# Modulation steps moved into the first dense product, and a quartered TensorE array for the RWKV pairs, in a hybrid RWKV-7 / mLSTM / PEER step

## The chip, the cores and the metric

The kernel runs on one core of a Trainium2 chip. The metric is the device time of one execution in microseconds (us), lower is better. The core has TensorE (PE, matrix products), VectorE (DVE), ScalarE (ACT), GpSimd (POOL) and SyncE (SP), which here only issues transfers. The engines run their own instruction streams in order and meet at semaphores.

## The reference

One layer of a decoder trunk on 288 tokens: 256 of a prompt and 8 sequences of 4 sample tokens. D is 2048. A conditioning vector c per sequence (9 in all) gives six modulation vectors for the layer and two for the end, each by a 2048 x 2048 matrix product.

```python
mod = silu(c) @ w_ada + b_ada          # six parts of 2048
sh_a, sc_a, g_a, sh_c, sc_c, g_c = split(mod, 6)
h = rmsnorm(x, g) * (1 + sc_a) + sh_a
z = h @ w_in                           # RWKV part, mLSTM q/k, mLSTM v/o/gates
y_a = rwkv7(z_a)                       # 16 heads of 64, delta rule, one step per token
y_b = mlstm(z_qk, z_rest)              # 4 heads, q/k 128 wide, v 256 wide
x += g_a * (concat(y_a, y_b) @ w_out)
h = rmsnorm(x, g2) * (1 + sc_c) + sh_c
x += g_c * peer(h)                     # 128 x 128 experts, top 16 in each of 8 heads
y = rmsnorm(x, g3) * (1 + sc_f) + sh_f # sh_f, sc_f from silu(c) @ w_ada_final
```

The RWKV step of a head is S = S diag(d) + (S (-kk)) (kk a)^T + v k^T, y = S r, with d the decay. Of the six modulation vectors only sh_a and sc_a are needed before the first product; g_a is needed after w_out, the others later still.

## The kernel before, in words

**Tiles and ring.** All weights come as tiles of 1 MB (128 partitions x 2048 words) through a ring of four slots. SyncE loads tile n when the semaphore `used` says that tile n - 4 has been used (`load`, `ada`). There are 32 modulation tiles at the front (parts SC_A and SH_A, 16 each), 50 tiles of w_in, 96 modulation tiles (G_A, SH_C, SC_C, G_C, SH_F, SC_F), 16 of w_out, 16 of w_q and 256 of the experts.

**A dense tile** (`dense`) multiplies a weight tile with 288 tokens in two halves of precision: ScalarE copies the tile to its high half (`hi`, two instructions), POOL subtracts that from the tile and gets the low half (`lo`, two instructions), and PE does 16 x 3 matmuls of 128 x 128 by 128 x 288 (high x high, high x low, low x high). In w_in the high halves have two buffers. ScalarE's queue has per tile: wait for the matmuls of tile j, `hi` of tile j + 2, then the copy of tile j out of its bank. For the first eight tiles (mLSTM q and k) the copy is followed by a wait for VectorE's convolution and a sigmoid. The loop over w_in has bodies of four tiles.

**A modulation step** (`ada_step`) takes one tile of 512 rows x 512 columns: 16 float32 matmuls with 32 columns of silu(c) as weights, in four column groups of the array. A float32 matmul stands in the trace as two records, so a step is 32 records. Four steps make a row of results that ScalarE copies out (`ada_take`); four such rows are folded to one part (`ada_turn`, 8 records) and stored (`ada_store`). The 96 deferred steps are put by hand, `ada_more(count)`, at places of the mLSTM and RWKV stages: 4 and 3 before the heads, 7 in each of four mLSTM heads, 11 until the RWKV pairs, 20 and 21 in the two pairs, 9 after them. PE's queue holds them in program order between the other matmuls.

**mLSTM heads.** For each head: products for the numerators (three banks), nine state updates (PE fills bank 4 or 5, VectorE takes it; update u waits for VectorE's update u - 2), the scores of the next head, and one sum of squares. The steps stood two after update 1, one after update 4, one after the scores, three after the sum.

**RWKV pairs.** The prompt has four chunks of 64 tokens, taken in two pairs: chunk j of a pair is on partitions 64j to 64j + 63, for all 16 heads. Grams and tokens come first; then the inverse of a triangular matrix per head by six levels of doubling:

```python
def times(bank, q, lhsT, rhs):        # heads 8q to 8q+7
    for h in range(8 * q, 8 * q + 8):
        for j in range(2):
            mm = matmul(ps[bank][PART[j], ...], lhsT[PART[j], h, :], rhs[PART[j], h, :])
```

A level is X = mask x Ti (`times` to banks 0 and 1), ScalarE's copies of X, then Ti += Tt X (banks 2 and 3) and Tt += X Tt (banks 0 and 1), added by VectorE in two halves of eight heads. Each `times` is 64 records for 16 heads. A head's matmul has its rows (its operands' partitions) and its columns (the partitions of its output) both in half j, so that two of the four quarters of the array are used, each pair of them writing the same bank. The products with AV (`akv`, `pu`) are placed alike. The products with PU (`mr`, state update, parts) take rows by chunk and columns by head. A step stood before and after the second half of every level.

POOL makes the mask of level i once level i - 2's X is done, and in the first pair three further products between them.

## Time and profile before

| | |
|---|---|
| median of 3 runs | 2926.09 us (2925.2 to 2926.27) |
| profiled execution | 2921.68 us, span 2919.9 us |
| PE busy | 2725.9 us of the span, 93% |
| POOL, VectorE, ScalarE busy | 1771.7, 1121.3, 951.9 us |
| read from and written to memory | 518.77 MB, 23.84 MB |
| granted PE clock, mean | 0.955 |

Stages, in us from the span's start: modulation parts 1 and 2 until 124; w_in 124 to 455; mLSTM until 618; preparation of the RWKV operands until 659; pairs 659 to 744 and 744 to 843; the sample tokens and the norm until 945; w_out and w_q until about 1175; the experts to the end. Granted clock 1.00 is 2.4 GHz and a mean between 0.5 and 1 mixes the two levels of 2.4 and 1.2 GHz.

How to read the rows below: a timeline row is start, duration, engine, line, instruction, out<-in with shapes, count, and in brackets the idle time before it with what ended it. PE rows carry `128*32` for the weights' shape; nearly all have line 701, the helper that issues a matmul. `kept` is the lower part of on-chip memory with the ring, `staged` the upper, `bank` a PSUM bank. "issue" means that the engine waited for nothing that the profile shows.

### The profile page before, as it was taken

How to read it: one execution, taken by the hardware profiler on the slowest of the kernel's cores; microseconds unless marked ns; L12 is line 12 of the kernel's file. 1: busy time of each engine (PE TensorE's matmuls, PEld its weight loads, DVE VectorE, ACT ScalarE, POOL GpSimd, SP SyncE). 2: the span in 40 equal slices, each digit the busy share in tenths (PEclk: the TensorE clock that was granted, in tenths of full speed). 3: DMA queues.
4: the chain of work that ended last, by engine and by line, in shares of the span. 5: the costliest groups of instructions: out<-in, count | busy, mean ns of one | idle time of the engine just before them, and what ended most of it. 6: DMA issues, size and time to landing. Idle time of an engine off the chain costs nothing.

```text
span 2919.9 us, 62759 instructions
## 1 busy us (share of the span) xinstructions
PE 2725.9 (93%) x25899; PEld 2620.6 (90%) x25899; DVE 1121.3 (38%) x2241; ACT 951.9 (33%) x1353; POOL 1771.7 (61%) x745
## 2 busy tenths in 40 slices
PE   5789999979875989999999999999999999999997
PEld 3689997768763979899999999999999999999997
DVE  0450664464237120896477313200131101455134
ACT  1343432131112333444333333333333333332333
POOL 0267771003211677688655577777777777888775
PEclk9899997679986999999999999999999999999999
DMA  9744445888664434344455444555544555554442
GB/s 374 263 142 165 165 160 212 290 294 285 233 208 162 159 126 162 130 158 158 174 182 181 164 171 159 179 185 187 177 159 172 184 182 189 185 183 174 169 163 104
DMA packets 150467, 544.94 MB, mean 187 GB/s; under 512 B 8984, under 2 KB 18856, under 8 KB 121512
## 3 DMA queue, kind: packets, MB, share of 16 engines
q1 hardware_dynamic: 136672, 505.18, 49.0%
q10 hardware_dynamic: 11480, 20.44, 1.9%
q0 software_dynamic: 2160, 17.03, 1.5%
q8 instruction: 125, 2.05, 0.3%
q14 instruction: 30, 0.25, 0.0%
HBM read 518.77 MB, written 23.84 MB: 186 GB/s over the span
## 4 chain that ended last, share of the span: by engine, by line
issue 39%; POOL 35%; PE 21%; DVE 3%; ACT 1%; POOLq 1%; DMA 0%; DVEq 0%; ACTq 0%
POOL ring_lo L605 34%; PE bank L701 21%; PE bank L704 0%; DVE staged L2106 0%; DVE y_lo L1758 0%; DMA kept<-in_w_ada 0%; POOLq L604 0%; DVE staged L2059 0%; ACT hi_peer L1337 0%; POOLq L609 0%; DVE staged L2093 0%; POOL h_lo L675 0%; POOL staged L694 0%; DVE staged L2095 0%; POOL staged L683 0%
## 5 line engine op out<-in xcount | busy, mean ns | idle before, releaser
L605 POOL TENSOR_TENSOR ring_lo<-kept,hi_peer 128x1024 fp32r<-128x1024 f32 x576 | 1441.6, 2526 | 496.9 <-ACT hi_peer L1337 496.9
L1337 ACT ACTIVATE hi_peer<-kept 128x1024 fp32r<-128x1024 f32 x576 | 578.1, 1051 | 1134.0 <-PE bank L701 1133.9
L701 PE MATMUL bank<-h_hi,ring_lo 128*128 128x288 f32 x3104 | 914.0, 294 | 0.0
L701 PE MATMUL bank<-h_hi,hi_peer 128*128 128x288 f32 x2304 | 686.1, 298 | 18.1 <-DVE h_lo L2152 10.3
L701 PE MATMUL bank<-h_lo,hi_peer 128*128 128x288 f32 x2304 | 680.7, 295 | 0.0
L701 PE MATMUL bank<-act_hi,hi_peer 128*128 128x288 f32 x2048 | 604.8, 295 | 6.7 <-POOL ring_lo L605 3.6
L701 PE MATMUL bank<-act_hi,ring_lo 128*128 128x288 f32 x2048 | 604.5, 295 | 0.0
L701 PE MATMUL bank<-act_lo,hi_peer 128*128 128x288 f32 x2048 | 604.2, 295 | 0.0
L701 PEld LDWEIGHTS bank<-h_hi,ring_lo 128*128 128x128 f32 x3104 | 585.8, 189 | 0.0
L701 PEld LDWEIGHTS bank<-h_hi,hi_peer 128*128 128x128 f32 x2304 | 432.4, 188 | 21.4 <-issue 16.2
L701 PEld LDWEIGHTS bank<-h_lo,hi_peer 128*128 128x128 f32 x2304 | 433.3, 188 | 0.0
L701 PEld LDWEIGHTS bank<-act_hi,hi_peer 128*128 128x128 f32 x2048 | 384.8, 188 | 8.4 <-POOL ring_lo L605 8.4
L701 PE MATMUL bank<-staged 64*64 64x64 f32 (+10 forms) x5264 | 339.9, 267 | 52.6 <-issue 18.3
L701 PEld LDWEIGHTS bank<-act_hi,ring_lo 128*128 128x128 f32 x2048 | 385.1, 188 | 0.0
L701 PEld LDWEIGHTS bank<-act_lo,hi_peer 128*128 128x128 f32 x2048 | 384.9, 188 | 0.0
L701 PEld LDWEIGHTS bank<-staged 64*64 64x64 f32 (+5 forms) x5264 | 283.3, 153 | 102.4 <-issue 51.8
L605 POOL TENSOR_TENSOR ring_lo<-kept,hi_front 128x1024 fp32r<-128x1024 f32 x100 | 243.3, 2453 | 205.1 <-ACT hi_front L1337 205.1
L2273 DVE CAST act_hi<-staged 128x576 fp32r<-128x576 f32 (+1 forms) x128 | 84.9, 663 | 578.1 <-PE bank L701 578.1
L701 PE MATMUL bank<-h_hi,hi_front 128*128 128x288 f32 x800 | 236.4, 296 | 11.4 <-POOL ring_lo L605 11.4
L701 PE MATMUL bank<-h_lo,hi_front 128*128 128x288 f32 x800 | 236.7, 296 | 0.0
L701 PE MATMUL bank<-kept,staged 128*32 128x128 f32 x4144 | 176.9, 328 | 64.0 <-DMA kept<-in_w_ada 36.9
L701 PEld LDWEIGHTS bank<-kept,staged 128*32 128x32 f32 x4144 | 137.9, 132 | 98.4 <-DMA kept<-in_w_ada 44.5
(219 smaller groups left out, 2371.0 us busy)
## 6 DMA issues: line engine op xcount, KB each, us to landing
kept<-in_peer_u SPq DMA_DIRECT2D x128, 1024.0 KB, 4.7
kept<-in_peer_v SPq DMA_DIRECT2D x128, 1024.0 KB, 5.5
kept<-in_w_ada SPq DMA_DIRECT2D x96, 1024.0 KB, 8.6
kept<-in_w_in SPq DMA_DIRECT2D x50, 1024.0 KB, 4.7
kept<-in_w_adaf SPq DMA_DIRECT2D x32, 1024.0 KB, 5.6
kept<-in_w_out SPq DMA_DIRECT2D x16, 1024.0 KB, 4.8
kept<-in_w_q SPq DMA_DIRECT2D x16, 1024.0 KB, 4.7
gates_spill<-staged ACTq DMA_DIRECT2D x24, 576.0 KB, 3.0
```

What stands on the lines that cost most here:

```text
L605: pool.tensor_tensor(ring_lo[:, n % RING_SLOTS, cols], ring[n % RING_SLOTS][:, cols], hi_slot(n)[:, cols].bitcast(F32), ALU.subtract).then ...
L701: return pe.matmul(out, lhsT, rhs, start=start, stop=stop)
L1337: return act.activation(out, in_, ACT.Copy)
L2273: dve.tensor_copy(act_hi[:, n % 2], a).then_inc(S("acts_hi"), 1)
```

## The change

First edit. Parts G_A and SH_C (32 tiles) leave the ring's later order and get two buffers of their own, `early`. Eight bodies of the w_in loop (now a loop of eight and one of four, where there were two of six) each take four steps: in the middle of tile 0, after tile 0, after tile 1, in the middle of tile 2; after tile 3 one fold of the row (`early_turn`). ScalarE takes the row before it waits for tile 3 (`early_take`). SyncE's queue interleaves the loads. 64 steps stay deferred: 2 in each head (5 fewer), 14 and 15 in the pairs (one per level, before the second half), the others as they were.

Second edit. In the pairs, heads are split into even and odd in place of lower and upper eight. For odd heads Ti, X-to-Tt products, AV and Tt have their chunks on the other half of the partitions (`side`), so that a product's output of an odd head lies in the other half from its operands, in a bank of its own. For this level 0 gets 16 matmuls with the unit matrix that bring the odd heads' mask over (into bank 3), and the last token turn becomes 12 matmuls where there were 4 transposes. X goes to banks 4 and 5. Both halves' waits are joined: a level's first product waits for both additions to Ti, the second for both copies of X. The products with PU go through their four combinations of chunk and head in the order `TILES`.

```diff
-        wg_hi, wg_lo = parts("wg_hi", za, KT, 36), parts("wg_lo", za + KT * 36, KT, 36)
+        early = [words(q5 + D + KT * N + b * D, D) for b in range(2)]
+        TILES = ((0, 0), (1, 1), (0, 1), (1, 0))
+        def side(h, j):
+            return PART[j ^ h % 2]
...
+            def load_early(q, body, i=0):
+                if q >= 2 or body or not isinstance(i, int):
+                    sp.wait_ge(S("early_used"), i * 4 + (4 * body + q - 1))
+                sp.dma_start(early[q % 2].rearrange("p (k c) -> p k c", k=4),
+                             T["w_ada"][q * 512:(q + 1) * 512, cols].rearrange("(k p) c -> p k c", p=P)
+                             ).then_inc(S(f"early{q % 2}_landed"), 16)
+            def load_body(z_j, z_at, body, last=False, i=0):
+                load_early(2, body, i)
+                load_z(z_j, z_at, i)
+                load_early(3, body, i)
+                load_z(z_j + 1, z_at + 1, i)
+                if not last:
+                    load_early(0, body + 1, i)
+                    load_early(1, body + 1, i)
+                load_z(z_j + 2, z_at + 2, i)
+                load_z(z_j + 3, z_at + 3, i)
...
+            def early_step(i, q):
+                pe.wait_ge(S(f"early{q % 2}_landed"), i * 32 + 16 * (q // 2 + 1))
+                if q == 0:
+                    pe.wait_ge(S("ada_copied"), i + 8)
+                for k_ in range(4):
+                    for g in range(4):
+                        mm = matmul(ps[6][32 * g:32 * g + 32, 0:P], silc[:, 4 * q + k_, :],
+                                    early[q % 2][:, k_ * 512 + g * P:k_ * 512 + (g + 1) * P],
+                                    q == k_ == 0, q == k_ == 3)
+                mm.then_inc(S("early_used"), 1)
+            def early_turn(i):
+                pe.wait_ge(S("ada_copied"), i + 9)
+                matmul(ps[7][:, bass.ds(i * (4 * NS), 4 * NS)], early_row, cst1("fold")).then_inc(S("ada_turned"), 1)
...
-            with pe.Fori(0, 6) as i:
+            with pe.Fori(0, EARLY_BODIES) as i:
                 for j in range(4):
                     pe.wait_ge(S("z_free"), i * 4 + (j + 1))
-                    dense(n_z + j, h_hi, h_lo, i, j % 2, "h")
+                    dense(n_z + j, h_hi, h_lo, i, j % 2, "h", {0: 0, 2: 3}.get(j))
+                    if j < 2:
+                        early_step(i, j + 1)
+                early_turn(i)
...
-                    if u in (1, 4):
-                        ada_more(2 if u == 1 else 1)
...
-                ada_more(3)
+                ada_more(1)
...
+                def times(bank, lhsT, rhs, rows, out, count):
+                    for h in range(AH):
+                        for j in range(2):
+                            mm = matmul(ps[bank + h % 2][out(h, j), (h // 2) * L:(h // 2 + 1) * L], lhsT[rows(h, j), h, :],
+                                        rhs[rows(h, j), h, :])
+                            if h >= AH - 2 and j == 1:
+                                mm.then_inc(S(count), 1)
...
+                    times(4, mk[i % 2], Ti, here, side, "x_sum")
+                    ada_more(1)
+                    pe.wait_ge(S("x_copied"), x_copies(p, i, 1))
+                    pe.wait_ge(S("t_added"), T_ADDS * p + 4 * i)
+                    if i < LEVELS - 1:
+                        times(2, Tt, X, side, here, "t_sum")
+                    times(0, X, Tt, side, side, "t_sum")
...
+            def early_take(i, first):
+                act.wait_ge(S("early_used"), i * 4 + 4 * (first + 1))
+                act.wait_ge(S("ada_turned"), i + (first + 5))
+                copy(early_row, ps[6][:, 0:P]).then_inc(S("ada_copied"), 1)
...
                 for j in range(4):
+                    if j == 3:
+                        early_take(i, 0)
                     act.wait_ge(used, i * 4 + (n_z + j + 1))
```

## Rows read from the trace of the kernel before

**Rows 1.** The page: busy tenths of PE and its granted clock, 40 slices of 73 us.
```profile
PE   5789999979875989999999999999999999999997
PEclk9899997679986999999999999999999999999999
```

**Rows 2.** Stretches: window, PE, PEld, DVE, ACT, POOL busy, PE clock, DMA share, GB/s.
```profile
199.00:455.20 256.20, 252.76 (x1921) 252.37 (x1921) 102.94 (x113) 100.04 (x177) 194.20 (x80) 1.00 0.46 164
522.40:555.00 32.60, 32.17 (x319) 24.51 (x315) 17.29 (x41) 5.01 (x9) 1.61 (x3) 0.69 0.89 322
659.00:744.00 85.00, 76.14 (x2214) 69.19 (x2216) 32.68 (x44) 14.87 (x29) 26.46 (x11) 0.94 0.78 264
700.00:721.00 21.00, 21.00 (x681) 19.41 (x678) 8.28 (x11) 4.14 (x8) 13.94 (x5) 1.00 0.77 258
744.00:843.00 99.00, 87.60 (x2410) 77.68 (x2406) 27.72 (x44) 18.93 (x39) 18.76 (x10) 0.95 0.69 227
868.00:880.00 12.00, 8.07 (x426) 6.83 (x416) 2.58 (x2) 1.27 (x5) 0.00 (x0) 0.80 0.06 18
1440.00:1480.00 40.00, 40.00 (x318) 40.00 (x317) 29.67 (x83) 14.04 (x24) 21.13 (x9) 1.00 0.50 183
```

**Rows 3.** Waits of PE, 124 to 205 us: total us, times, longest.
```profile
PE bank L701 <- POOL ring_lo L605: 9.3, 7, 2.7
```

**Rows 4.** Timeline of ScalarE in the convolution tiles.
```profile
156.24 1.99 ACT L1337 ACTIVATE hi_front<-kept 128x1024 fp32r<-128x1024 f32 x2
...
163.69 0.46 ACT L1334 ACTIVATE staged<-staged 128x312 f32<-128x312 f32 x1 [4.99 <-DVE staged L1807]
...
165.47 1.06 ACT L1337 ACTIVATE hi_front<-kept 128x1024 fp32r<-128x1024 f32 x1
```

**Rows 5.** Timeline of the second mLSTM head: modulation steps, an update by VectorE, a fold.
```profile
533.36 3.64 PE L701 MATMUL bank<-kept,staged 128*32 128x128 f32 x64
...
536.09 0.48 DVE L1936 SCALAR_TENSOR_TENSOR staged<-staged,bank 128x256 f32<-128x256 f32 x1
...
540.00 1.94 PE L701 MATMUL bank<-kept,staged 128*32 128x128 f32 x32
...
550.54 1.95 PE L701 MATMUL bank<-kept,staged 128*32 128x128 f32 x64
...
552.43 1.08 PE L701 MATMUL bank<-staged 128*128 128x36 f32 x8
```

**Rows 6.** Waits of PE, 455 to 945 us: total us, times, longest.
```profile
PE bank L701 <- issue: 27.8, 19, 4.7
...
PE bank L701 <- DMA kept<-in_w_ada: 5.8, 2, 5.2
```

**Rows 7.** Timeline of PE after the pairs.
```profile
871.22 1.92 PE L701 MATMUL bank<-staged 64*32 64x64 f32 x128 [0.37 <-issue]
874.70 1.84 PE L701 MATMUL bank<-staged 64*32 64x64 f32 x128 [1.56 <-issue]
```

**Rows 8.** PE's instruction queue, 659 to 744 and 1400 to 1600 us: packets, MB, share.
```profile
q8 instruction: 17, 0.28, 1.3%
...
q8 instruction: 4, 0.07, 0.1%
```

**Rows 9.** Timeline of PE in the first pair: step, products by times, state update.
```profile
693.12 1.08 PE L701 MATMUL bank<-kept,staged 128*32 128x128 f32 x32
694.13 2.08 PE L701 MATMUL bank<-staged 64*64 64x64 f32 x64
...
697.16 3.95 PE L701 MATMUL bank<-staged 64*64 64x64 f32 x128
...
702.05 2.08 PE L701 MATMUL bank<-staged 64*64 64x64 f32 x64
...
735.13 2.02 PE L701 MATMUL bank<-staged 64*64 64x64 f32 x117 [1.29 <-issue]
```

**Rows 10.** The page's transfers of w_ada: count, KB each, us to landing.
```profile
kept<-in_w_ada SPq DMA_DIRECT2D x96, 1024.0 KB, 8.6
```

More of the change, by code:

```diff
@@ L503, in parts_turned, with parts_stored @@
         def parts_turned(j):
-            return j + 4 if j else 1
+            return j + 10 if j else 1
+        def parts_stored(j):
+            return j + 3 if j else 1
+        EARLY_BODIES = 8
         ada_places = []
@@ L738, in ada_step @@
                 mm.then_inc(used, 1)
-                if quarter == 0 and j > 0 and j != 2 and q == 3:
+                if quarter == 0 and (j == 1 or j > 4) and q == 3:
                     ada_turn(j - 1)
@@ L752, in ada_more, with dense @@
                     ada_step(*pending.pop(0))
-            def dense(n, hi, lo, i, bank, split=None):
+            def dense(n, hi, lo, i, bank, split=None, middle=None):
                 w_hi, w_lo = hi_slot(n), ring_lo[:, n % RING_SLOTS]
                 for kt in range(KT):
+                    if kt == 8 and middle is not None:
+                        early_step(i, middle)
                     if kt % 8 == 0:
@@ L1047, in _ @@
+                    for j, hp in TILES:
+                        h = 2 * f + hp
+                        out = ps[2 + j][PART[hp], f * AHD:(f + 1) * AHD]
+                        mm = matmul(out, ktok2[PART[j], h, :], vtok2[PART[j], h, :], False, p == j == 0 and f == MT - 1)
                 if p == 0:
                     mm.then_inc(S("step_ready"), 1)
-                else:
-                    pe.wait_ge(S("rk_taken"), MT)
                 ada_more(1)
@@ L1355, in ada_store @@
                      turn_bank(j)[:, 0:KT * NS]).then_inc(S("mods_raw"), 1)
-            pending = [(j, q) for j in range(2, 8) for q in range(4)]
+            pending = [(j, q) for j in range(4, 8) for q in range(4)]
             ada_steps = [0]
@@ L1474, in take_z @@
                 copy(zxs[:, j % 2, :, 0], src).then_inc(S("zx_full"), 1)
-            with act.Fori(0, 6) as i:
+            with act.Fori(0, 2) as i:
+                for j in range(4):
+                    if j == 3:
+                        early_take(i, 6)
+                    take_z(i, j, j)
+            act.wait_ge(S("ada_turned"), 13)
+            copy(mods[:, G_A:G_A + 2].rearrange("p m k s -> p (m k s)"), ps[7][:, 0:2 * KT * NS]).then_inc(S("mods_raw"), 1)
+            with act.Fori(2, 6) as i:
                 for j in range(4):
@@ L1561, in _ @@
                         act.wait_ge(S("x_sum"), x_sums(p, i, q))
[L1562 removed]
+                        copy(X[:, q::2], ps[4 + q][:, :].rearrange("p (h t) -> p h t", h=8)).then_inc(S("x_copied"), 1)
                     if p == 1 and i >= 2:
```

229 lines of the change are left out of this document (124 added, 105 removed).

## The prediction

> **What bounds the kernel now.** The page comes first: TensorE (PE) is busy nearly throughout, with a dip between 455 and 945 us (slices 7 to 13 of 40, 73 us each), where the granted clock also falls [rows 1]. The table of stretches then splits the front half [rows 2]. The sum is made against the profiled execution, 2921.68 us (span 2919.9); the median of the runs, 2926.09 us, stands 4.4 us above it, and I add that back at the end.
>
> In the first dense product (124 to 455.2 us, 50 tiles) PE is the bound except in its first 75 us: from 199 to 455.2 it is idle 3.4 of 256.2 us, at full clock, with the DMA engines 46% busy [rows 2]. In the first 75 us, the eight convolution tiles, PE waits seven times for the low halves of the weights, 9.3 us in all [rows 3]. What is late there is ScalarE: it can take the next tile's high half only after the previous tile's sigmoid, which waits 5.0 us for VectorE. Its loop takes 7.9 us per tile (it starts a high half at 156.24 and ends the sigmoid of that turn at 164.16) [rows 4], against 6.3 us of matmuls (later in the stage 1921 records fill 252.8 us, 0.132 each, 48 to a tile [rows 2]).
>
> In the mLSTM heads (488 to 618 us, some 32.5 us each) PE is busy but mostly at half clock (0.69 in the second head) [rows 2]. The row of one head shows what a modulation step costs: two in a row 3.64 us at half clock, one alone 1.94, two at full clock 1.95 [rows 5].
>
> In the two RWKV pairs (659 to 843 us) PE is nearly saturated, with gaps that the view calls issue: 27.8 us of them in 455 to 945, 19 times, the largest cause in this stretch; the transfers of w_ada cost PE only 5.8 us [rows 6]. I read the issue gaps as instruction fetch, and two rows show its floor: two runs of exactly 128 matmul records start 3.48 us apart, though each ran only 1.92 and 1.84 us, with a gap of 1.56 between, in a stretch where the DMA engines are 6% busy [rows 2, 7]. The first pair issues 2214 matmul records while PE's instruction queue brings 17 packets, 130 records to a packet [rows 2, 8]. I call 128 records a page (256 instructions, with their weight loads): fetch supplies a page in no less than about 3.45 us.
>
> **The first edit: 32 of the 96 steps move.** Each dense body of four tiles gets four steps and one small fold; eight bodies.
> Price of a step: one at full clock between other work starts 1.01 us before what follows it (693.12 to 694.13) [rows 9].
> - Bodies 2 to 7 lie where PE never waits. 24 x 1.01 = 24.2 us, all on the path. The fold is two records; eight of them take 1.08 us [rows 5], so 6 x 0.27 = 1.6.
> - Bodies 0 and 1 lie where PE has 9.3 us of waits. Eight steps (8.1) fit, but the fold waits for ScalarE's copy of the finished row, which stands behind the third tile's sigmoid in ScalarE's queue. ScalarE starts its turn for the fourth tile at 156.24; PE's fourth tile should be through at about 149.5 (its high half starts two turns earlier, near 140.5, and POOL's two subtractions and the second half of the matmuls end some 9 us after that). So PE stands there about 7 us, with the fifth tile behind it, and then finds both halves of that tile ready. It catches up before ScalarE needs it: tile 4 ends near 164.2 and ScalarE turns to it at 165.47. Going through both bodies like this, tile 10 ends about 5.2 us later than now, four of which are body 2's own steps. I charge 1.2 us.
> - Transfers: SyncE's queue gets four more loads of 1 MB per body, interleaved with the weights. A body then moves 8.39 MB in 4 x 6.3 + 4.3 = 29.5 us, 284 GB/s; the table shows 322 GB/s in the second head [rows 2]. A weight tile has two tiles of time (12.6 us) between its load and ScalarE's first read of it; even the w_ada loads of now land in a median of 8.6 us [rows 10]. The tightest early tile is asked for at the middle of tile 0 and used after tile 1, some 10.5 us later. I take nothing, and keep the shortfall as a rival. POOL's queue is not touched; ScalarE gets eight copies of 0.28 us, hidden where it is not the bound.
> Sum for the dense stage: +27 us. Bounds: 22 (7 of the 9.3 us hide, steps at the 0.94 us that they take in a row) and 34 (each step 0.2 us dearer, for emptying the array at both changes of shape, and no cover).
>
> The Trainium skill, TensorEngine Tiling (Array Packing), section Tiling Modes, says that changing the tiling mode drains TensorE. No row prices a drain inside a dense tile; the difference between 1.01 and 0.94 us is what this trace shows of it, and by the page's rule the sum would lie nearer the 34.
>
> **What leaves the heads** (5 of 7 steps in each of four). The two steps after the first two updates cover a wait that stays: the third update needs VectorE's first, which it starts only at 536.09 and which needs a second small instruction behind its 0.48 us, while PE would be free at 533.36 [rows 5]. Worth nothing. The step after the fifth update (1.94 us) has no wait behind it, and two of the three at the tail (0.98 each, full clock) have none either, since the next head's scores are ready before. 4 x (1.94 + 1.95) = 15.6, I take 16. Below, 12: the lighter load keeps the clock low. Above, 22: the shorter tail carries the high clock further into the next head.
> With 20 tiles fewer asked for, the ring is full at the end of the heads: the 5.8 us of waits for w_ada go, and with them the cold steps behind the 5.22 us one (1.94 us at half clock against 1.08). -8 (5 to 11).
>
> **The pairs.** Three things change. One of two steps per level goes (6 per pair, 192 records each pair). The products by `times`, `akv` and `pu` use four quarters of the array instead of two. Level 0 gets 32 records by the unit matrix, the last token turns 16 more records per half.
> What four quarters give: two-quarter products take 3.95 us per 128 records, 30.9 ns each; the state update, whose order already visits all four, takes 2.02 us for 117, 17.3 ns [rows 9]. If nothing else bound, a full level would go from 7.92 us (694.13 to 702.05 [rows 9]) to 1.1 + 1.0 + 2.2 plus two waits that one step no longer hides, about 0.5 each, for ScalarE's two copies and VectorE's two additions: 5.3 us.
> But a level still has 64 + 32 + 128 = 224 records, 1.75 pages, and fetch gives a page in 3.45 us at best, so 6.0 us. The first pair now takes 85 us for 2214 records, 17.3 pages: 4.9 us per page; the second 99 for 2410, 18.8 pages: 5.3 [rows 2]. After: 192 - 32 - 32 = 128 records fewer in each, exactly one page. From 700 to 721 a page took 3.95 us without a gap under 77% DMA [rows 2]. I take 3.95 for the first pair (16.3 x 3.95 = 64, and 6 for waits on VectorE: 70, -15) and 4.3 for the second (17.8 x 4.3 + 6 = 82.5, -16). Together -31. Bounds: -10 if pages keep today's pace (one page each), -40 if the dependence alone decides.
>
> **Sum.** +27 - 16 - 8 - 31 = -28. Profiled 2921.7 - 28 = 2894; as a median 2926.1 - 28 = **2898 us**. What follows 843 us is unchanged. The likeliest case's own range is 2872 to 2914.
>
> **Rivals.** Less than about 0.2% (6 us) can't be told from no change here.
> 1. Fetch eats the second edit: pages keep 4.9 and 5.3 us, the pairs give 10 only, net -7: 2919 us. For it: 19 gaps of some 1.5 us stand in the middle stages [rows 6], under 69% DMA in the second pair. Against: 3.95 us held for 21 us, and halving the steps eases the DMA engines. A part of this is that the quarters don't run side by side (the change doesn't do what it says); the update's 17.3 ns speaks against that. Chance 0.18.
> 2. The dense loop no longer fits PE's instruction store. Its body grows from 384 to 640 matmul and weight-load instructions, two and a half pages. If each of seven returns to the loop's head waits for a page, 7 x 3.5 to 5.3 us, up to 37: net -4 to +9, about 2929. Against: the loop with the gates (4 x (96 + 48) = 576 instructions, 2.25 pages) runs from 1400 to 1600 us with four instruction packets in the whole 200 us [rows 8], and PE is busy in 40 of the 40 us of one pass [rows 2]. Chance 0.07.
> 3. The other side: the early tiles come too late. The dense stage is fed at 164 GB/s now. If the mixture with w_ada reached only the 227 GB/s of the second pair, a body would take 37 us, not 29.5: 6 x 7.8 = 47 on top, net +19, 2945 us. It decides from the point where six bodies lose 28 us, 34.2 us a body or 245 GB/s. Against: 322 GB/s with the same tiles in a later stretch. Chance 0.07.
> 4. More than forecast: pairs -40, heads -22 with full clock, dense +24: below 2872. Chance 0.05.
> That leaves 0.63 for the forecast.
>
> The Trainium skill, Runtime: NRT & Kernel Launch, section Instruction fetch mechanics, says that a taken branch whose target lies outside a window of two pages forces a fetch; by that rule rival 2 would be the outcome. The same section gives PE an instruction memory of 2048 instructions, by which it would not. The four packets of the gates' loop side with the second.
>
> **Chances and range.** Faster by over 0.2%: the forecast, rival 4 and a good half of rival 1, 0.78. Within 0.2%: the rest of rival 1 and part of 2, 0.09. Slower: most of 2 and rival 3, 0.13. The range of 8 in 10 runs from 2868 to rival 1 with 2 us to spare, 2921.
>
> **What would show it.** Right: the dense stage ends about 27 us later, with no DMA waits in it and 32 groups of 32 records among the dense ones; the second head shorter by 4 us with a new wait of some 3.5 us for VectorE before the third update; no wait for w_ada near 614; `times` at 16 to 20 ns a record with issue gaps that fill part of what that saves; the pairs near 70 and 83 us. Wrong: instruction packets in the dense stage, waits for the early tiles, pairs above 80 and 94 us, or a half clock in the dense bodies.

## The result and the profile after

The changed kernel takes 2941.08 us (median of 13 runs, 2929.75 to 2944.91), the kernel before 2924.11 us beside it: a ratio of 1.0057, 95% interval 1.0047 to 1.0067. It is slower by 17 us where I had forecast 28 us less. Of all the executions in this document one, of experiment 1, ran in a slow state (3071.55 us, against 2921.57 to 2925.73 for its eleven others), and its ratio leaves that one out. The profiled execution has a span of 2938.9 us, 19.0 more than before, and the stages below split those 19.0 us.

The page of the changed kernel, busy tenths of PE and its clock, in 40 slices of 73.5 us, answers to [rows 1]; PE is less busy in the slice where the first pair begins (the tenth, 7 tenths for 9), and the clock is lower in slices 9 to 11 (6, 8 and 8 tenths for 7, 9 and 9).

```profile
PE   4799999887875989999999999999999999999997
...
PEclk9899998668886999999999999999999999999999
```

Four rows of the changed kernel answer to [rows 2]: the stretch of the dense product, most of the one between it and the pairs, and each pair from its first gram to its last product (window, busy us and instructions of PE, PEld, DVE, ACT, POOL, PE clock, DMA share, GB/s).

```profile
200.00:492.00 292.00, 292.00 (x2774) 283.35 (x2774) 100.40 (x118) 104.15 (x188) 195.20 (x80) 1.00 0.66 227
492.00:660.00 168.00, 144.76 (x1070) 106.98 (x1070) 84.17 (x181) 31.82 (x60) 8.80 (x16) 0.64 0.48 174
681.27:768.39 87.12, 71.44 (x2129) 62.65 (x2129) 30.76 (x42) 14.26 (x28) 26.43 (x11) 0.86 0.57 186
768.39:859.02 90.63, 76.08 (x2277) 65.52 (x2273) 27.75 (x43) 17.71 (x37) 19.95 (x10) 0.92 0.56 177
```

The kernel before, cut at the same places of its pairs:

```profile
660.29:745.22 84.93, 77.36 (x2249) 70.11 (x2249) 31.47 (x42) 15.46 (x30) 26.46 (x11) 0.94 0.78 265
745.22:844.05 98.83, 87.43 (x2404) 77.54 (x2401) 28.69 (x43) 18.93 (x39) 19.81 (x10) 0.95 0.68 226
```

PE's busy time in the pairs falls from 164.8 to 147.5 us, but its idle time rises from 19.0 to 30.2 us, and the first pair runs at a clock of 0.86 instead of 0.94. By stage, after less before:

| stage | before | after | difference | forecast |
|---|---|---|---|---|
| end of the dense product | 455.2 | 491.9 | +36.7 | +27 |
| from there to the first gram of the pairs | 205.1 | 189.4 | -15.7 | -24 |
| both pairs | 183.8 | 177.8 | -6.0 | -31 |
| from there to w_out's first matmul (944.58, 962.48) | 100.5 | 103.5 | +2.9 | 0 |
| rest | | | +1.1 | 0 |

The waits of PE from 120 to 500 us, changed kernel (total us, times, longest), answer to [rows 3]: ScalarE has taken POOL's place.

```profile
PE bank L747 <- ACT staged L1421: 8.3, 3, 3.0
```

Its timeline there: the wait of the first fold, in ScalarE's queue behind a sigmoid that waits for VectorE. ScalarE's copy of the fold row is the one at 157.40.

```profile
157.81 0.41 PE L747 MATMUL bank<-staged 128*128 128x36 f32 x2 [2.98 <-ACT staged L1421]
```
```profile
157.03 0.46 ACT L1418 ACTIVATE staged<-staged 128x312 f32<-128x312 f32 x1 [5.02 <-DVE staged L1907]
157.40 0.26 ACT L1421 ACTIVATE staged<-bank 128x128 f32<-128x128 f32 x1
```

A step inside a dense tile, changed kernel. Dense records follow one another 0.13 us apart; here the second record after the step starts 1.48 us after the last one before it, so the step costs 1.48 - 2 x 0.13 = 1.22 us. That is 1.01 us for the step itself (211.82 to 212.83) and 0.10 and 0.11 at its two ends, where the starts lie 0.23 and 0.24 us apart.

```profile
211.46 0.29 PE L747 MATMUL bank<-h_lo,hi_front 128*128 128x288 f32 x1
211.59 0.29 PE L747 MATMUL bank<-h_hi,ring_lo 128*128 128x288 f32 x1
211.82 1.08 PE L747 MATMUL bank<-staged 128*32 128x128 f32 x32
212.83 0.40 PE L747 MATMUL bank<-h_hi,hi_front 128*128 128x288 f32 x1
213.07 0.29 PE L747 MATMUL bank<-h_lo,hi_front 128*128 128x288 f32 x1
```

The waits of PE from 500 to 680 us: VectorE before each head's third update, as forecast, and w_ada, which was forecast to go.

```profile
PE bank L747 <- DVE staged L2037: 12.3, 4, 3.3
PE bank L747 <- DMA kept<-in_w_ada: 4.7, 1, 4.7
```

And the timeline of PE in the pairs of the changed kernel: the last token turn (with two steps in its group), the gaps, and what runs behind one.

```profile
692.37 6.99 PE L747 MATMUL bank<-kept,staged 128*128 128x64 f32 x112 [0.20 <-ACT staged L1421]
...
719.20 3.02 PE L747 MATMUL bank<-staged 64*64 64x64 f32 x128 [0.57 <-issue]
724.85 1.08 PE L747 MATMUL bank<-staged 64*64 64x64 f32 x45 [2.62 <-issue]
725.86 1.93 PE L747 MATMUL bank<-kept,staged 128*32 128x128 f32 x32
...
818.68 1.16 PE L747 MATMUL bank<-staged 64*64 64x64 f32 x64 [0.59 <-ACT staged L1421]
```

The quarters are faster, but not in every product: 64 records in 1.16 us are 18 ns each, and the two products behind them 3.02 us for 128, 23.6 ns, against 30.9 [rows 9]. These two are unlike, and the code says why:

```python
                    if i < LEVELS - 1:
                        times(2, Tt, X, side, here, "t_sum")
                    times(0, X, Tt, side, side, "t_sum")
```

The last two places before the name of the semaphore are the partitions of the operands and of the output. In `X Tt` an odd head's output lies in the same half as its operands, like an even head's. So this product still uses two quarters (as does the first product of level 0, by `here` for both), and the text on the second edit, which has a product's output of an odd head in the other half, does not hold for it. The trace shows it. The stretch of experiment 5 that has no gap splits into 0.98 us for the 64 records of `Tt X` and 1.84 us for those of `X Tt`, by the starts 15.3 and 28.8 ns a record. In experiment 8, with two quarters everywhere, the same two take 29.9 and 28.8. (Records that run over a cut are counted on both sides of it.)

```profile
711.76:712.74 0.98, 0.98 (x65) 0.98 (x66) 0.00 (x0) 0.00 (x0) 0.98 (x2) 1.00 1.04 408
712.74:714.58 1.84, 1.84 (x77) 1.84 (x68) 1.28 (x2) 0.00 (x0) 1.44 (x1) 1.00 0.33 124
```

And a page of 128 records that ran 3.02 us is followed by a gap of 2.62 us and then by a step at half clock (1.93 us, against 1.08 elsewhere).

### The profile page after: what moved, and what is told of

The parts are those of the page before. It is cut to its first block, busy times and chain, and to the rows that moved or that the text cites. A ratio compares the mean times of both kernels' runs of the same rounds, so it can differ in the third digit from the quotient of the medians.

```text
span 2938.9 us, 63158 instructions
## 1 busy us (share of the span) xinstructions
PE 2726.2 (93%) x26043; PEld 2613.6 (89%) x26043; DVE 1117.7 (38%) x2241; ACT 950.1 (32%) x1352; POOL 1772.5 (60%) x745
## 4 chain that ended last, share of the span: by engine, by line
issue 32%; POOL 31%; PE 26%; DVE 5%; DMA 3%; ACT 1%; POOLq 1%; SPq 0%; ACTq 0%; DVEq 0%
POOL ring_lo L651 31%; PE bank L747 26%; DMA kept<-in_w_ada 3%; DVE staged L1907 1%; ACT staged L1421 0%; DVE staged L2209 0%; PE bank L750 0%; ACT hi_front L1421 0%; DVE y_lo L1858 0%; DVE staged L1844 0%; POOLq L650 0%; DMA kept<-in_w_in 0%; DVE staged L2022 0%; DVE staged L2162 0%; ACT hi_peer L1421 0%
## 5 line engine op out<-in xcount | busy, mean ns | idle before, releaser
L747 PE MATMUL bank<-staged 64*64 64x64 f32 (+11 forms) x6352 | 361.1, 275 | 82.4 <-issue 29.7
L747 PEld LDWEIGHTS bank<-staged 64*64 64x64 f32 (+6 forms) x6352 | 296.6, 152 | 141.2 <-issue 75.0
L747 PE MATMUL bank<-kept,staged 128*32 128x128 f32 (+2 forms) x3216 | 150.5, 335 | 64.7 <-DMA kept<-in_w_ada 39.1
L1421 ACT ACTIVATE staged<-bank 128x384 f32<-128x384 f32 (+7 forms) x281 | 105.8, 417 | 288.1 <-PE bank L747 269.4
```

What stands on the lines that cost most here:

```text
L747: return pe.matmul(out, lhsT, rhs, start=start, stop=stop)
L1421: return act.activation(out, in_, ACT.Copy)
```

## The experiments

All ratios are to the kernel before, run beside on the same chip; the chips and the runs beside differ from experiment to experiment, so a difference of two medians can be off by some 3 us from that of the ratios. "Pairs" are the two spans from the profile of each, that is from one execution, cut as in the tables above.

**1 and 2. One edit at a time.** The first edit alone keeps the pairs of before, with one step per level (64 steps are left to place); the second alone keeps all 96 steps.

```diff
@@ first edit alone, against the changed kernel
-                    times(4, mk[i % 2], Ti, here, side, "x_sum")
+                        times(q, q, mk[i % 2], Ti).then_inc(S("x_sum"), 1)
...
@@ second edit alone, against the changed kernel
-            with pe.Fori(0, EARLY_BODIES) as i:
+            with pe.Fori(0, 6) as i:
                 for j in range(4):
-                    dense(n_z + j, h_hi, h_lo, i, j % 2, "h", {0: 0, 2: 3}.get(j))
+                    dense(n_z + j, h_hi, h_lo, i, j % 2, "h")
...
-                        ada_more(1)
+                        ada_more(2)
```

> The change with its second edit undone: steps beside the dense tiles, one step per level in the pairs, products on two quarters as before. The profile after has the dense stage 36.7 us longer and the stretch from its end to the first gram 15.7 us shorter. Theory F (fetch takes the second edit's gain): the pairs lose only the 12 steps, about three pages of instructions of 4.9 to 5.3 us, so 182.5 us go to about 170, and the total is the before plus 36.7 - 15.7 - 12 + 1 = +10 us. So the second edit by itself would cost some 6 us. Rival Q (the quarters do save what the matmul rate says, some 25 us, and something of the first edit costs it back): the pairs stay near 182 - 12 + 25 = 195 us and the total is +35 us.

Measured: 2923.61 against 2922.85 us, 1.0005 (0.9997 to 1.0014). Pairs 75.7 and 84.0 us.

> The kernel before with the second edit alone: all 96 deferred steps where they were, 7 in a head and two per level, products on four quarters. The dense stage and the heads should be as before to 1 us. Theory F: pages of instructions keep their pace, the pairs have 64 records each more than before (half a page) and the dearer token turn (2.4 us a pair in the profile after), so the pairs go from 182.5 to 183 to 190 us, total +1 to +8. Rival Q: 25 us saved, total -20 us.

Measured: 2940.53 us, 1.0057 (1.0043 to 1.0070). Pairs 96.5 and 105.9 us, in the slowest of its six executions (2946.41). The waits of PE, 655 to 870 us: the kernel before, the first edit alone, the second alone.

```profile
PE bank L701 <- issue: 23.6, 14, 4.7
```
```profile
PE bank L746 <- issue: 18.7, 13, 4.7
```
```profile
PE bank L702 <- issue: 33.2, 18, 3.3
```

So the second edit makes the whole loss, 18 us in the pairs, and it does so with the first edit (159.8 to 177.8) as without it (183.8 to 202.4; by the medians 17.5 and 17.7 us). The first edit is neutral: the 12 steps that leave the pairs give back 24 us there, two each, and not one. Both expectations for the second edit missed: one had it near nothing, the other at a gain.

**3. The fold row is taken early.** ScalarE copies the finished row right after it has handed the third tile to VectorE, before it waits for VectorE.

```diff
                 for j in range(4):
-                    if j == 3:
-                        early_take(i, 0)
...
                          conv0[:, bass.ds(i * 4 + j, 1)].rearrange("p o b t -> p (o b) t")).then_inc(S("zq_full"), 1)
+                    if j == 2:
+                        early_take(i, 0)
                     act.wait_ge(S("conv_ready"), i * 4 + (j + 1))
```

> The change with one thing moved: in the convolution tiles ScalarE copies the finished row in its turn for tile 2, ahead of the wait for VectorE's convolution, not at the head of its turn for tile 3. If the two waits of 3.0 us before the fold, and the half clock behind them (tile 8 took 3.1 us too long), cost what they look like, the dense stage ends 4 to 8 us earlier than in the change (its end at 491.9 us goes to 484 to 488) and the total is 4 to 8 us lower. Rival: ScalarE's loop is the bound there anyway, the time shows again as a wait for low halves, and only the cold 3 us come back, or nothing.

Measured: 2927.33 us, 1.0016 (1.0007 to 1.0025), 13.8 us less than the changed kernel by the medians and 12 us by the ratios (1.0057); the dense product ends at 481.2 instead of 491.9 and the first gram starts at 669.88 instead of 681.27. More than expected. The waits of PE, 120 to 500 us, now read:

```profile
PE bank L747 <- ACT staged L1421: 2.3, 1, 2.3
```

The two fold waits are gone, 6.0 us; the rest is what they did to the clock. In the changed kernel the first half of the tile behind each takes 4.8 and 5.8 us, with the row taken early 3.25 and 3.3, and the window up to 200 us has a clock of 0.91; with the row taken early it is 0.97:

```profile
120.00:200.00 80.00, 78.06 (x809) 73.43 (x810) 46.30 (x65) 32.06 (x58) 44.39 (x19) 0.97 0.77 269
```

**4. A quarter of the deferred loads.** Three of four loads of the 64 deferred tiles are left out; each step reads the quarter's one tile, so the modulations made from these tiles are not the reference's. Instructions on PE are the same.

```diff
-                    for q in range(4):
+                    for q in range(4 if j < 2 else 1):
...
-                n = ada_tile(j, quarter) + q
+                n = ada_tile(j, quarter) + (q if j < 2 else 0)
```

> The change, but of every four tiles of the 64 deferred modulation steps only one is loaded and used four times (three quarters of the rows of these weights are left out of the modulation vectors). PE issues the same instructions; the transfers of the middle stages fall from 67 to 17 MB. Theory L (instruction pages are late because they stand behind weight transfers): gaps called issue in the pairs shrink from some 30 us to below 12, a page comes in 3.5 us, and the pairs go from 177.7 to 155 to 162 us. Rival G (a page has a fixed latency of its own, or something else spaces it): the gaps stay, the pairs stay within 5 us. Either way the 4.7 us wait for w_ada at 640 goes.

Measured: 2909.11 us, 0.9961 (0.9948 to 0.9975). The wait for w_ada is gone and the first gram comes 5.5 us earlier (675.79); the pairs take 71.2 and 83.9 us with the DMA engines 16% and 20% busy. Theory L had the pairs right and the gaps wrong: the gaps called issue in 655 to 870 us add up to 19.7 us instead of 27.9, not to less than 12. Of the 22.7 us that the pairs lose, 12.2 are idle time of PE and 10.4 busy time, at a clock of 0.98 and 0.96 instead of 0.86 and 0.92. Two timelines show the same two products, 128 records in 3.02 us, and the start of what follows: with full loads (719.20 above) 5.65 us later, and here 4.00.

```profile
708.19 3.02 PE L747 MATMUL bank<-staged 64*64 64x64 f32 x128 [0.58 <-issue]
712.19 0.92 PE L747 MATMUL bank<-staged 64*64 64x64 f32 x45 [0.98 <-issue]
```

The same place in the second pair gives 5.91 us (795.61 to 801.52) and 3.72 (772.96 to 776.68).

The trace also has the time of every packet of PE's instruction queue, and these times tie the gaps to it. In the pairs of the changed kernel 17 gaps are called issue, and each of them ends 1.2 to 1.5 us after such a packet has landed; of this experiment's 17 in the pairs each ends 1.2 to 1.6 us after one. For the gap that ends at 724.85 the packet ran from 722.53 to 723.48, for the one at 712.19 from 709.81 to 710.69. The packet itself takes about 1.0 us in both kernels. What differs is when it starts: 3.3 and 3.6 us after the 128 records have begun (719.20, 795.61) under full loads, 1.6 and 1.1 us after (708.19, 772.96) under a quarter of them. So the gaps are instruction supply, and the transfers of w_ada slow it; at these places they delay the start of a packet, not its transfer.

**5 and 6. Four levels of the first pair, unrolled and in a loop.** In both, levels 1 to 4 go without their step (the four steps stand together behind them) and get four short matmuls that carry the waits; in one the four levels are written out, in the other they are two passes of a loop over two levels.

```diff
+                    pe.wait_ge(S("t_added"), it * 8 + (4 * (i - 1) + 3))
+                    carrier(4)
+                    times(4, mk[i % 2], Ti, here, side, "x_sum")
...
+                    with pe.Fori(0, 2) as it:
+                        for i in (1, 2):
+                            level(i, it)
+                    ada_more(4)
```

> The change, with the four steps of levels 1 to 4 of the first pair put behind level 4, and four small extra matmuls per level that carry the waits: the control for the next kernel, all instructions of the four levels written out. If fetch bounds them, the four levels (832 records, 6.5 pages with the extra ones) take 4.3 to 4.9 us a page, 28 to 32 us, with gaps called issue of 1 to 3 us each one or two pages. If the dependence through ScalarE and VectorE bounds them, they take about 4 x 5.5 = 22 us with waits on ScalarE and VectorE in place of the gaps.

> As the control, but levels 1 and 2 of the first pair are the body of a hardware loop that runs twice, so that the second pass (levels 3 and 4) needs no instructions from memory. Matmuls, waits, banks and transfers are the same. Theory F: the second pass has no issue gaps and takes about 2 x 5.5 = 11 us, against 14 to 16 in the control; the kernel is 3 to 6 us faster than the control. Rival D (dependence, not fetch): both passes take what they take in the control. Rival B: the return to the loop's head costs a gap of its own of 2 to 4 us.

Measured: unrolled 2939.54 us, 1.0065 (1.0039 to 1.0091); looped 2937.08, 1.0055 (1.0039 to 1.0072). The 2.5 us between them lie inside the intervals. The timelines say why there is nothing to gain: already unrolled, a level without a step has no issue gap, and yet the next one starts 6.92 us later, with waits for ScalarE (the copies of X) and VectorE (the additions).

```profile
711.20 0.62 PE L747 MATMUL bank<-kept,staged 128*32 128x128 f32 x4 [1.17 <-ACT staged L1447]
711.76 3.02 PE L747 MATMUL bank<-staged 64*64 64x64 f32 x128
714.70 0.41 PE L747 MATMUL bank<-kept,staged 128*32 128x128 f32 x2
715.45 0.41 PE L747 MATMUL bank<-kept,staged 128*32 128x128 f32 x2 [0.34 <-DVE staged L2143]
...
718.12 0.62 PE L747 MATMUL bank<-kept,staged 128*32 128x128 f32 x4 [1.17 <-ACT staged L1447]
```

These 6.9 us hold 0.9 us that the carriers put on the path: two of the four stand there for 0.56 us before the products (711.20 to 711.76) and the last for 0.33 us before the next level's first product (715.45 to 715.78). Without them a level is some 6.0 us, by my estimate: 1.2 for the first product, 1.2 until ScalarE's copies are done, 2.9 for the other two products, 0.75 until VectorE's additions are done. That, and not the 5.3 us of the prediction, is what the dependence of a level costs here. The loop could not show what supply costs, because its control had no gap left in these levels.

**7. The first edit alone with the fold row taken early.** Edit 3 on the kernel of experiment 1.

> The first edit alone (the pairs as before the change, but one step per level), with ScalarE's copy of the finished fold row moved ahead of its wait for VectorE in the two convolution bodies. The first edit alone came out at 1.0005 of the kernel before, and the move took 13.5 us off the changed kernel. If the two effects are independent, this one is 12 us faster than the kernel before (ratio 0.996), with pairs of about 76 and 84 us. Rival: the 13.5 us came partly from how the second edit's pairs met the transfers; then the move gives 4 to 8 us here and the ratio is 0.998.

Measured: 2911.4 us, 0.9966 (0.9953 to 0.9979), pairs 75.1 and 82.4 us. It is the fastest of all that compute the reference, 11.5 us under the kernel before, as the sum of the two effects said.

**8. Two quarters, same instructions.** On the kernel of experiment 3, the odd heads' products return to the partitions of the even ones (the products by the unit matrix in level 0 in the same way, not shown); number, order, waits and banks stay.

```diff
         def side(h, j):
-            return PART[j ^ h % 2]
+            return PART[j]
...
-    matmul(ps[4 + half][PART[1 - j], at + L:at + P], src[:, f, ct[j]], ident[:, L:P])
+    matmul(ps[4 + half][PART[j], at + L:at + P], src[:, f, ct[j]], ident[:, L:P])
```

> The changed kernel with the fold row taken early (2927 us, 1.0016), but every product of the odd heads is written on the same partitions as in the kernel before: number, order, waits and banks of all instructions stay those of the second edit, only the two products of a head with different result quarters become two with the same two quarters for all heads. Theory A (page supply sets the pace, the four quarters save nothing net): within 4 us of 2927, products by times at 31 ns a record instead of 18, issue gaps in 655 to 870 us down from 31 us to about 20, pairs of 84 to 89 us still. Rival B (the four quarters themselves lose the time, through the gaps and the half clock behind them): 8 us or more faster. Rival C (the four quarters do pay, the other parts of the second edit cost 30 us): 10 to 20 us slower.

Measured: 2928.57 us, 1.0020 (1.0007 to 1.0033), 1.2 us more than with four quarters, well inside the intervals. The gaps called issue in 655 to 870 us are 15.4 us instead of 31.2, fewer than the 20 expected. The pairs of the two, four quarters first:

```profile
669.88:754.90 85.02, 70.05 (x2129) 61.60 (x2129) 30.68 (x42) 14.26 (x28) 26.47 (x11) 0.88 0.59 190
754.90:843.48 88.58, 72.94 (x2277) 62.35 (x2273) 27.75 (x43) 17.71 (x37) 19.80 (x10) 0.98 0.58 181
```
```profile
670.20:758.11 87.91, 76.99 (x2128) 68.93 (x2128) 30.67 (x42) 14.26 (x28) 26.43 (x11) 0.94 0.57 186
758.11:849.99 91.88, 82.97 (x2276) 73.73 (x2272) 27.74 (x43) 17.71 (x37) 19.75 (x10) 0.96 0.55 173
```

The quarters take 17.0 us of busy time out of the pairs and put 10.8 us of idle time in; 6 us are left in these two profiles, 1 in the medians. Theory A.

**9. Two quarters, plain turns.** As 8, and the last token turn goes back to transposes (48 records become 8, not the 16 that I had counted: a transpose is one record here).

```diff
-                            if u < 3:
+                            if u <= 3:
                                 mm = turn(ps[4 + half][:, at:at + P], src[:, f, pt])
```

> As the one above, and the last token turn goes back to 16 matmul records by transposes (the 48 records of three matmuls per column block are gone). The turn's group took 6.99 us for 112 records, 64 of them two steps of 1.96 us, so 5.0 us against 2.5 us for the transposes: 5 us faster than the one above for two pairs if only its own records count (theory A), up to 10 us if it runs at half clock as in the second edit alone (9.39 us for the group) and its page no longer has to be fetched. If nothing (within 2 us), the turn was hidden by the supply of pages.

Measured: 2918.45 us, 0.9993 (0.9977 to 1.0009): 10 us less than experiment 8, pairs 82.1 and 89.8 us. The turn that moves the odd heads to their own partitions costs ten microseconds for two pairs, and its own records account for them. From the start of the turn to the end of the two steps behind it 8.58 and 6.92 us pass in experiment 8, and 2.96 us twice in experiment 9, 9.6 us less. Experiment 8, then the turn and the steps of the first pair in experiment 9:

```profile
679.75 8.65 PE L747 MATMUL bank<-kept,staged 128*128 128x64 f32 x112 [0.20 <-ACT staged L1421]
...
767.66 6.99 PE L747 MATMUL bank<-kept,staged 128*128 128x64 f32 x112 [0.20 <-ACT staged L1421]
```
```profile
679.58 1.15 PE L750 MATMUL bank<-kept,staged 128*128 128x128 f32 x8 [0.20 <-ACT staged L1421]
680.65 1.95 PE L747 MATMUL bank<-kept,staged 128*32 128x128 f32 x64
```

The expectation had set 5.0 us for the turn against 2.5 for the transposes. The transposes take 1.07 us (679.58 to 680.65), and the turn's group is 1.7 us longer where the clock falls in it (0.80 in the first pair, 1.00 in the second).

What is left of the second edit here (the other order of waits and of products, the other banks, 32 records of the unit matrix per pair) is 7 us against experiment 7 by the medians. The profiles say 14 us in the pairs, but the profiled execution here is the slowest of its twelve (2923.99). In the second pair the steps follow one another about 9.1 us apart instead of 8.0, and a wait for ScalarE stands in each level that shares its banks with the rk sums:

```profile
788.97 2.28 PE L747 MATMUL bank<-staged 64*64 64x64 f32 x64 [0.59 <-ACT staged L1421]
791.18 1.08 PE L747 MATMUL bank<-kept,staged 128*32 128x128 f32 x32
...
798.02 1.15 PE L747 MATMUL bank<-staged 64*64 64x64 f32 x32 [0.59 <-ACT staged L1421]
```

**10 and 11. The same pairs under a quarter of the loads.** The cut of experiment 4 on the first edit alone, and on the changed kernel with two quarters (outputs as there).

> The first edit alone, with three of four loads of the 64 deferred tiles left out (each step reads the quarter's one tile, so the output is not the reference's). To be held against the same cut in the changed kernel, 2909.1 us, pairs of 71.2 and 83.9 us. Theory A (pages come slower when the DMA engines are loaded, 5 us against 3.5 to 4.0 at 18% share, and the second edit costs its own extra records and colder turns whatever the load): pairs of 66 to 72 and 74 to 80 us, 2900 us or less. Rival (with cheap pages the four quarters pay): pairs longer than those of the changed kernel, 2915 us or more.

> The changed kernel with three of four loads of the 64 deferred tiles left out (2909.1 us, pairs of 71.2 and 83.9 us; output not the reference's), and the odd heads' products on the same partitions as the even ones', as in the run with two quarters and the same instructions. Theory A (the quarters pay only where pages come fast; under full load they gave nothing, 2928.6 against 2927.3): 5 to 12 us slower, pairs of 75 to 80 and 86 to 90 us. Rival N (the quarters pay nothing even then, waits between the engines eat them): within 3 us of 2909.

Measured: the first edit alone 2907.13 us, 0.9945 (0.9928 to 0.9962), pairs 72.3 and 81.9; the changed kernel with two quarters 2920.89 us, 0.9994 (0.9985 to 1.0003), pairs 80.5 and 88.6, against 2909.11 with four. Experiment 10 fell between its two expectations: with light loads the second edit costs 2 us by the medians and 4.7 by the ratios, where with full loads it costs 16 to 18. Experiment 11 says which part of it depends on the loads: four quarters (in all products but `X Tt`) are worth 11.8 us by the medians and 9.6 by the ratios when pages come fast, and 1.2 us, which can't be told from nothing, when they don't. Their pairs, four quarters first:

```profile
675.79:746.98 71.19, 63.79 (x2128) 55.95 (x2128) 30.58 (x42) 14.26 (x28) 26.50 (x11) 0.98 0.16 49
746.98:830.88 83.90, 73.29 (x2277) 63.02 (x2273) 27.73 (x43) 17.71 (x37) 19.80 (x10) 0.96 0.20 62
```
```profile
674.89:755.41 80.52, 76.14 (x2128) 68.87 (x2128) 30.64 (x42) 14.26 (x28) 26.45 (x11) 0.94 0.14 43
755.41:844.04 88.63, 81.62 (x2276) 72.43 (x2272) 27.74 (x43) 17.72 (x37) 19.77 (x10) 0.98 0.20 59
```

Busy time falls by 20.7 us and idle time rises by 6.6: the pairs keep 14.1 of it.

**12. The turn on quarters.** On experiment 3, the turn's matmuls use only the 64 partitions on which the head lies.

```diff
-    matmul(ps[4 + half][:, at:at + L], src[:, f, pt], ident[:, 0:L])
+    matmul(ps[4 + half][:, at:at + L], src[PART[0], f, pt], ident[PART[0], 0:L])
-    mm = matmul(ps[4 + half][PART[1 - j], at + L:at + P], src[:, f, ct[j]], ident[:, L:P])
+    mm = matmul(ps[4 + half][PART[1 - j], at + L:at + P], src[PART[1], f, ct[j]], ident[PART[1], L:P])
```

> The changed kernel with the fold row taken early (2927 us), four quarters kept, and the 48 records of the last token turn written as products that use only the 64 partitions on which a head lies: 16 on half of the array's rows and 32 on a quarter. Same number of records and instructions. In the two-quarter version the way back to 16 transposes gave 10 us. Theory T (the turn is dear because its matmuls run on whole columns, some 0.1 to 0.2 us each, and chill the clock): the group of 112 records falls from about 7 to 9 us to 4 us, and the kernel by 6 to 10 us, to 2917 to 2921 us; it stays above the 2911 us of the first edit with the early row, since the four quarters save nothing there. Rival S (what the way back to transposes gave was the 32 records fewer, a quarter of a page): group shorter, but the pairs within 2 us of 85.0 and 88.6 us.

Measured: 2930.1 us, 1.0025 (1.0013 to 1.0038), 2.8 us more than experiment 3, not 6 to 10 less. Both theories missed: the group of 112 records still takes 8.56 and 9.86 us, and the pairs 91.1 and 92.6 us, in an execution at the slow end of its eight (2934.59).

```profile
679.64 8.56 PE L747 MATMUL bank<-kept,staged 64*128 64x64 f32 x112 [0.20 <-ACT staged L1421]
```

In the changed kernel the 48 records of a turn take 5.0 us at full clock, 105 ns each. The six of a block start 0.16, 0.21, 0.01, 0.10, 0.01 and 0.15 us apart, and here, on 64 partitions, just the same to 0.01 us. The 0.21 stands behind the product with 128 columns and the 0.15 ahead of the next one, the others have 64; no run took these changes away, so why the turn is dear stays open. Its share of the array is not the reason.

## Why the prediction was wrong

**Dense stage, bodies 2 to 7: mechanism right, size off.** The term was 24 x 1.01 + 1.6 = 25.8 us. The folds of the changed kernel stand 30.24 us apart, and four tiles of before take 192 x 0.1316 = 25.27 [rows 2], so a body gained 4.97 us and six of them 29.8. The price of a step there is 1.22 us, not 1.01: some 0.1 us at each change between whole and narrow columns. It lies inside the bound of 34. The Trainium skill, TensorEngine Tiling (Array Packing), section Tiling Modes, has it that a change of tiling mode drains TensorE; I had kept it for the upper bound only, and the trace agrees that the change costs something, 0.21 us a step.

**Bodies 0 and 1: the step that failed first.** I wrote that PE stands some 7 us at the fold, finds both halves of the next tile ready and catches up, and charged 1.2 us. Measured: 36.7 - 29.8 = 6.9 us at the end of the dense product. With the row taken early (experiment 3) it ends 10.7 us sooner, 25.9 us after that of the kernel before, so that the two bodies then give back 3.9 us. The waits were shorter than I thought, 2.98 us twice, 6.0 of the 10.7. What I left out is the clock: the work with which PE was to catch up ran partly at half speed behind each wait, 4.0 us in the two half tiles.

**The loops.** Rival 2 did not come: between 124 and 492 us PE's instruction queue brings 5 packets, though the dense body is more than 640 instructions long. The page of the Trainium skill that I weighed, Runtime: NRT & Kernel Launch, section Instruction fetch mechanics, fits this stage with its 2048 instructions and not with its window of two pages. Rival 3 did not come either: no wait for a transfer in the stage, at 227 GB/s with every tile in time.

**Heads: right.** The third updates stand 28.4, 28.5 and 27.6 us apart (541.91, 570.30, 598.80, 626.43) instead of some 32.5, so four heads give the 16 forecast or a little more, with the new wait for VectorE before the third update (3.31 us in three heads, 2.39 in the last).

**The w_ada wait: wrong.** I let 8 us go because the ring would be full, and even its rows give only 5.8 + 0.9 = 6.7. The wait of 4.74 us stays (645.15), at the fifth step of a row of five that takes 11 us, while the ring has four slots and a load lands in 8.8 us. That fewer tiles had been asked for before did not help; the wait was gone only with three of four deferred loads left out (experiment 4).

**Pairs: the step that decided.** -31 was forecast, -6 came, and of the two parts of the forecast one was too small and the other had the wrong sign. The 12 steps that leave give 24 us (experiment 1). I read this as 1 us of work and a quarter of a page to fetch for each, but their transfers leave with them, and no run separates the three. The second edit costs 18 us. Its failing step is "I take 3.95 for the first pair and 4.3 for the second": I took pages at 3.95 us without a gap [rows 2] as a proof that supply can do that, while they only show that work as long as that hides it. With work of 3.0 us a page, the next page came after 5.65 and 5.91 us. So the faster products turned into gaps (10.8 of 17.0 us, experiment 8). That gaps also cost clock shows in single rows (the 1.93 us step) and in the first pair, 0.88 with four quarters against 0.94 with two, but not in the second, 0.98 against 0.96. The second failing step is the level that would take 5.3 us if nothing else bound it: it takes some 6.0 (experiments 5 and 6), since `X Tt` stayed on two quarters at 28.8 ns a record where I had put 17 for both products. With ten such products that is some 9 us of work too few in the forecast, by my estimate; the run that puts them on four quarters is missing. And the third is that the token turn was counted as records of a page, at nothing of its own: it costs 10 us (experiment 9). Its records were miscounted as well, 40 more in a pair and not 32 (2249 to 2129 in the first pair is 120 fewer, where I had 128).

Rival 1 named the mechanism, with a chance of 0.18, but priced it as the absence of a gain. It also asked whether the quarters run side by side and let the update's 17.3 ns answer for all products, where `X Tt` had needed a look of its own. It could not see a loss, because it priced the new instructions at the pace of the old ones. 2941 us lies outside every case but rival 3, and its cause is not rival 3's.

What stays open: how far ahead PE fetches, since twelve pages of before came 4.42 us apart with one gap, of 1.29 us, under 74% DMA share; what makes the records of the turn take 105 ns; what the second edit is worth with `X Tt` on four quarters; and how the last 7 us (experiment 9 against 7) divide between the order of waits and the product by the unit matrix.

## What to carry to other kernels

Where straight-line code of short matmuls runs at its supply of instructions, a faster instruction buys a gap; first take instructions out of the stretch, or bulk transfers, and only then make each one faster. A gap-free stretch gives a bound on supply from one side only. And before a wait is called covered, look at the engine's queue: a copy of 0.26 us moved ahead of another engine's wait gave 12 us here, 6 of them the two waits and most of the rest clock. Last, when products are to be spread over parts of the array, write down rows and output for each of them, and read the time of each by itself: a mean of 23.6 ns hid one product at 15 and one at 29.

## What the runs showed of the hardware that I had not expected

- Two waits of 2.98 us cost 10.7 us at the end of the stage and 12 us in the whole kernel by the ratios: the granted clock from 120 to 200 us was 0.91 with them and 0.97 without.
- A gap called issue in the pairs ended 1.2 to 1.6 us after a packet of PE's instruction queue had landed, in all 34 cases of the changed kernel and of the one with a quarter of the loads; the packet took 1.0 us.
- The same 128 matmul records, 3.02 us of work: the next page followed 5.65 us after their start with the DMA engines at 55% of that stretch, 4.00 us with them at 1%. The changed kernel, then the one with a quarter of the loads:

```profile
719.20:724.85 5.65, 3.02 (x128) 2.88 (x128) 3.97 (x5) 0.00 (x0) 0.27 (x1) 1.00 0.55 182
```
```profile
708.19:712.19 4.00, 3.02 (x129) 2.89 (x128) 2.67 (x5) 0.00 (x0) 0.00 (x0) 1.00 0.01 4
```

- A change between matmuls on whole columns and on 32 columns costs 0.10 to 0.11 us each way in a dense stream that otherwise has none (1.22 us for a step against 1.01).
- 64x64 products on four quarters ran at 15.3 ns a record, start to start, and on two quarters at 28.8 to 29.9.
